# Norms of the delta rule as per-token scalars, its gate columns beside the rotary key, and two PSUM banks held in the RWKV scan

## What is computed

```python
q = l2_normalize(q) * 64 ** -0.5         # x * rsqrt(sum(x*x) + 1e-6), per token and head
k = l2_normalize(k)                      # 8 heads of 64
beta = sigmoid(gb); g = -exp(a_log) * softplus(ga + dt_bias)
gc = cumsum(g)                           # inside a chunk of 64 tokens
lhs = strict(einsum(k * beta, k) * exp(gc_i - gc_j)) + I
u, w = solve(lhs, v * beta), solve(lhs, k * beta * exp(gc))
o = einsum(q * exp(gc), S) + einsum(incl(q k^T * decay), v_new)
o = rms_norm(o, norm_w) * silu(gz)       # eps 1e-6, over 64
```

## Time and profile before

| | us |
|---|---|
| median of 3 runs (4081.65 to 4089.67) | 4083.42 |
| the profiled execution | 4090.37 |
| its span, first to last instruction | 4088.6 |

### The profile page before, as it was taken

How to read it: one execution, slowest core, us unless ns; L and a number is a source line. 1 busy time by engine, 2 the same in 40 slices (tenths; PEclk the granted TensorE clock), 3 DMA queues, 4 the chain that set the end, 5 groups by cost and what they waited for, 6 DMA issues and landing times.

```text
span 4088.6 us, 71017 instructions
## 1 busy us (share of the span) xinstructions
PE 3896.2 (95%) x30810; PEld 3170.3 (78%) x30810; DVE 2103.5 (51%) x2922; ACT 1309.5 (32%) x1891; POOL 144.6 (4%) x193
## 2 busy tenths in 40 slices
PE   8998978999999999999989999999999998999998
PEld 5766768887778888888768688887888767688887
DVE  4977466755444445334755453345333746553335
ACT  4253333213323323222422532223222332532222
POOL 0000012220000000000000000000000000000000
PEclk8999878999999999999999999999999989999999
DMA  6213000023342223333102032322323201123331
GB/s 253 71 63 99 7 2 3 3 72 140 124 134 99 93 97 99 103 93 103 53 3 82 11 109 93 103 98 88 103 93 104 63 12 57 37 88 103 93 103 52
DMA packets 319751, 327.81 MB, mean 80 GB/s; under 512 B 10064, under 2 KB 243552, under 8 KB 318032
## 3 DMA queue, kind: packets, MB, share of 16 engines
q1 hardware_dynamic: 312144, 287.01, 21.9%
q0 software_dynamic: 7296, 36.27, 2.4%
HBM read 314.86 MB, written 8.39 MB: 79 GB/s over the span
## 4 chain that ended last, share of the span: by engine, by line
PE 74%; issue 12%; DVE 9%; ACT 3%; DMA 1%; POOL 0%; DVEq 0%; ACTq 0%; SPq 0%; POOLq 0%
PE psum L247 72%; DVE arena L301 2%; PE psum L254 2%; ACT arena L351 1%; DVE arena L312 1%; DVE ring L301 1%; DVE r L301 1%; DVE ring L332 1%; ACT r L351 1%; ACT ring L351 1%; DVE arena L332 1%; DMA ring<-in_w_ada 0%; DVE ring L308 0%; DVE arena L316 0%; DVE arena L306 0%
## 5 line engine op out<-in xcount | busy, mean ns | idle before, releaser
L247 PE MATMUL psum<-r 128*128 128x512 f32 (+2 forms) x12960 | 2847.6, 381 | 30.6 <-DVE r L301 28.4
L247 PEld LDWEIGHTS psum<-r 128*128 128x128 f32 x12960 | 2343.7, 188 | 521.2 <-DVE r L301 28.5
L301 DVE TENSOR_TENSOR r<-ring,r 128x2048 fp32r<-128x2048 f32 (+2 forms) x261 | 573.7, 2198 | 322.3 <-ACT r L351 318.7
L351 ACT ACTIVATE r<-ring 128x2048 fp32r<-128x2048 f32 (+2 forms) x261 | 478.6, 1834 | 362.9 <-PE psum L247 310.4
L351 ACT ACTIVATE arena<-psum 128x512 f32<-128x512 f32 (+7 forms) x509 | 268.1, 527 | 999.5 <-PE psum L247 923.5
L247 PE MATMUL psum<-arena 64*64 64x64 f32 (+11 forms) x5854 | 486.6, 271 | 35.0 <-DVE arena L301 9.7
L247 PEld LDWEIGHTS psum<-arena 64*64 64x64 f32 (+5 forms) x5854 | 313.9, 155 | 175.9 <-issue 100.4
L301 DVE TENSOR_TENSOR arena<-arena,psum 128x512 f32<-128x512 f32 (+4 forms) x217 | 136.3, 628 | 582.5 <-PE psum L247 563.5
L247 PE MATMUL psum<-ring 64*64 64x64 f32 (+3 forms) x7792 | 302.5, 232 | 44.7 <-DVE ring L332 12.8
L247 PEld LDWEIGHTS psum<-ring 64*64 64x64 f32 (+2 forms) x7792 | 262.0, 142 | 68.8 <-issue 30.8
L351 ACT ACTIVATE r<-arena 128x512 fp32r<-128x512 f32 (+1 forms) x176 | 109.4, 622 | 503.0 <-DVE arena L301 500.8
(11 more groups left out here) (113 smaller groups left out, 1532.3 us busy)
## 6 DMA issues: line engine op xcount, KB each, us to landing
ring<-in_ffa_w_in SPq DMA_DIRECT2D x88, 512.0 KB, 4.7
ring<-in_ffb_w_in SPq DMA_DIRECT2D x88, 512.0 KB, 4.7
ring<-in_w_mlp SPq DMA_DIRECT2D x32, 1024.0 KB, 5.2
ring<-in_w_in SPq DMA_DIRECT2D x31, 1024.0 KB, 5.2
ring<-in_w_ada SPq DMA_DIRECT2D x24, 1024.0 KB, 5.2
ring<-in_mix_w_in SPq DMA_DIRECT2D x24, 1024.0 KB, 5.1
ring<-in_ffa_w_out SPq DMA_DIRECT2D x20, 1024.0 KB, 4.9
ring<-in_ffb_w_out SPq DMA_DIRECT2D x20, 1024.0 KB, 5.0
```

What stands on the lines that cost most here:

```text
L247: ins = self.raw.matmul(o, l, r, start=start, stop=stop, skip_group_check=True)
L301: self.done(self.raw and self.raw.tensor_tensor(o, a, b, f), keys)
L351: self.done(self.raw and self.raw.activation(o, i, f, scale=scale, bias=bias), keys)
```

## The change

1. **RWKV scan.** `K.held` is a set of banks that `take` passes over. From A's take until the tile's inverse begins, A's two banks are in it.
2. **Norms as scalars.** q and k stay unnormed. The squares are summed with the squares as the stationary side and a 128x2 table as the moving one, so the sums come per token (`m.sums`). ScalarE takes `lk` = ln(sum of k) and `rk` = exp(-lk/2). `rk` goes into beta's factor, `-lk/2` into the decay's exponents on the key's side (by a product with the new constant `steps` and two small operations), and q's norm into the epsilon of the output's norm (`m.eq`). The head table's transposes, the root, the reciprocal, `to_all` and `dve_mx_scale` go.
3. **Gate columns beside the rotary key.** One chunk `abkr` of 128 columns holds the 16 gate columns and the 64 of the rotary key; its 24 products stand where the gates' were. VectorE does the rotary there. The product `kr2` and its chunk go, and one `E.ahead()` on ScalarE and on VectorE with it.

```diff
     def take(self, *key, among=BANKS):
-        b = next(b for b in K.order if b in among)
+        b = next(b for b in K.order if b in among and b not in K.held)
...
+def rw_held(K, d, pos):
+
+    return {K.bank_of[f"rw{d}", "A", pos, g][0] for g in range(2)}
...
         o = [t.take(st, "A", pos, g) for g in range(2)]
+        K.held |= rw_held(K, d, pos)
...
     for pos in range(6):
+        K.held -= rw_held(K, d, pos)
         yield from pe_invert(t, K, f"rw{d}", K.m.rw[d].sets[pos % 2], pos, (f"rw{d}", "AT sb", pos))
...
 def pe_mx_in(E, K, l):
-    for q in (0, 1):
-        o = t.take("mx hb", l, q)
-        for i in range(4):
-            f = 4 * q + i
-            t.tr(o[0:16, 128 * i:128 * i + 128], C["hs"][:, 16 * f:16 * f + 16], *([("mx hb", l, q)] if i == 3 else []))
...
-            t.mm(sums[0:16, :], C["hs"][:, 16 * f:16 * f + 16], m.tmp2[f % 2], f == 0, f == 7, ("mx sums", l, f))
+            for i in range(4):
+                t.mm(sums[:, 16 * i + 2 * f:16 * i + 2 * f + 2], m.tmp2[f % 2][:, 128 * i:128 * i + 128], C["b2"][:, 0:2],
+                     True, True, *([("mx sums", l, f)] if i == 3 else []))
...
-    i, wh, wl = t.chunk(W, 0, 8, 2048, 16)
+    i, wh, wl = t.chunk(K.I["abkr"][l], 0, 8, 0, 128)
...
-    def to_all():
-        z = [K.bank_of[("mx z", l), 0, i][0] for i in range(4)]
-        for f in range(8):
-            o = t.take("mx rn", l, f, among=tuple(b for b in BANKS if b not in z))
-            t.wait_ge(*K.at("mx rn", l))
-            t.mm(o, m.hb[0:16, 128 * f:128 * f + 128], m.rn[0:16], True, True, ("mx rn b", l, f))
...
-    pe_tm(t, K, ("mx z", l), W, 1536, 512, 8, m.hL, W512, within=to_all, late=lambda: pe_gates(E, K, l))
+    pe_tm(t, K, ("mx z", l), W, 1536, 512, 8, m.hL, W512, late=lambda: pe_gates(E, K, l))
...
 def act_mx_in(E, K, l):
-    a.wait_ge(*K.at("mx sums sb", l))
-    a.act(m.rn[0:16], m.rn[0:16], ACT.Sqrt, ("mx sd", l))
...
 def dve_mx_in(E, K, l):
     v.wait_ge(*K.at("mx sums", l, 7))
-    v.ts(m.rn[0:16], K.bank("mx sums", l)[0:16, :], 1e-6, None, ADD, None, ("mx sums sb", l))
+    v.ts(view(m.sums, [1, 64]), K.bank("mx sums", l)[:, 0:64], 1e-6, None, ADD, None, ("mx sums sb", l))
...
-    v.recip(m.rn[0:16], m.rn[0:16], ("mx rn", l))
+    v.ts(m.eq, m.sums[:, :, 0:8], 64e-6, None, MUL, None)
+    v.wait_ge(*K.at("mx ab", l))
+    dve_rotary(v, m.tmp, m, m.krT[RP, :], K.bank("mx ab", l))
...
 def pool_gates(E, K, l):
+    g.load(m.steps, K.I["steps"], "steps", l)
...
 def dve_gates(E, K, l):
-    v.ts(m.ng, m.gg, -1.0, None, MUL, None)
+    v.wait_ge(*K.at("gd be", l))
+    v.tt(m.rk, m.rk, m.be, MUL)
...
 def dve_gates2(E, K, l):
-    v.tt(view(m.kde, [1, 32]), K.bank("gd gc", l)[:, 32:64], view(m.t8, [1, 32]), SUB, ("gd kde raw", l))
+    v.tt(view(m.kde, [1, 32]), K.bank("gd gc", l)[:, 32:64], view(m.t8, [1, 32]), SUB)
+    v.stt(m.kde, m.lk, -0.5, m.kde, MUL, ADD, ("gd kde raw", l))
+    v.stt(view(m.ng, [1, 32]), K.bank("gd gc", l)[:, 64:96], -0.5, view(m.gg, [1, 32]), MUL, SUB)
...
 def act_gates(E, K, l):
+    a.wait_ge(*K.at("mx sums sb", l))
+    a.act(m.lk, m.sums[:, :, 8:16], ACT.Ln, ("gd lk", l))
+    a.act(m.rk, m.lk, ACT.Exp, scale=-0.5)
...
 def pe_gates(E, K, l):
+    t.wait_ge(*K.at("gd lk", l))
+    t.wait_ge(*K.at("in", "steps", l))
+    t.mm(o[:, 64:96], m.steps, view(m.lk, [1, 32]), True, True, ("gd gc mm", l))
...
-    t.wait_ge(*K.at("mx qk", l, 7))
...
 def pe_sb_in(E, K, l):
-    i, wh, wl = t.chunk(K.I["kr2"][l], 0, 8, 0, 128)
-    o = t.take("sb kr", l)
-    for k in range(8):
-        t.mm3(o, wh[:, k, :], wl[:, k, :], m.hL[:, 0, k, :], m.hL[:, 1, k, :], k == 0, k == 7,
-              *([("sb kr", l), ("w used", i)] if k == 7 else []))
...
 def dve_sb_in(E, K, l):
-    E.ahead()
     dve_mla_squares(E, K, l, "c", m.ckv, m.small[:, 4:8], ("mla n", l, "var"))
     dve_mla_norm(E, K, l)
     E.ahead()
-    v.wait_ge(*K.at("sb kr", l))
-    dve_rotary(v, m, m.krT[RP, :], K.bank("sb kr", l))
```

More of the change, by code:

```diff
@@ L118, in __init__ @@
         self.psum = ctx.enter_context(nc.psum_tensor("psum", [128, 8, 512], F32))
-        self.operands, self.r = set(), {}
+        self.operands, self.r, self.held = set(), {}, set()
         self.restart()
@@ L922, in memory @@
     m.cv = view(al(1024), [512, 2], [1, 512])
-    m.rn, m.abT = al(512), al(512)
-    m.hb = view(m.ktok, [1, 1024])
+    m.steps = al(128)
+    al(384)
+    m.abT = al(512)
     A.top = mk6 + 336
     m.Og = view(al(2048), [512, 4], [1, 512])
-    A.top += 1024
+    m.sums = view(al(64), [16, 4], [1, 16])
+    m.lk, m.rk, m.eq = (view(al(32), [8, 4], [1, 8]) for _ in range(3))
+    A.top += 1024 - 160
     m.al_, m.dtb = al(8), al(8)
@@ L3079, in act_mx_in @@
     a.copy(m.abT[0:16], K.bank("mx ab", l)[0:16, :], ("mx ab sb", l))
-    K.free(a, "mx ab", l)
+    K.free(a, "mx ab", l, part="act")
     to_tokens(11)
-    a.wait_ge(*K.at("mx sums sb", l))
-    a.act(m.rn[0:16], m.rn[0:16], ACT.Sqrt, ("mx sd", l))
     for _ in tm_walk(E, 512, 8, 4):
@@ L3128, in dve_mx_in @@
         pass
-def dve_mx_scale(E, K, l):
-    v, m = VectorLine(E, "mx"), K.m
-    for f in range(8):
-        v.wait_ge(*K.at("mx rn b", l, f))
-        x, pv = m.qk[:, f, :], K.bank("mx rn", l, f)
-        if f < 4:
-            v.stt(x, x, 0.125, pv, MUL, MUL)
-        else:
-            v.tt(x, x, pv, MUL, ("mx qk", l, f))
-        K.free(v, "mx rn", l, f)
 def pool_gates(E, K, l):
@@ L3219, in pe_gates @@
     t.mm(o[:, 0:32], C["UI"], view(m.gg, [1, 32]), True, True)
[L3220 removed]
+    t.mm(o[:, 32:64], C["blk"], view(m.gg, [1, 32]), True, True)
+    t.wait_ge(*K.at("gd lk", l))
+    t.wait_ge(*K.at("in", "steps", l))
+    t.mm(o[:, 64:96], m.steps, view(m.lk, [1, 32]), True, True, ("gd gc mm", l))
     o = t.take("gd egl", l, among=others)
@@ L3525, in dve_gd_squares @@
         v.red(m.small[:, 8 * i:8 * i + 8], h8(m.tmp2[i % 2]), ADD)
-    v.ts(m.small[:, 0:32], m.small[:, 0:32], 1.0 / 64, 1e-6, MUL, ADD, ("gd n", l, "var"))
+    v.stt(m.small[:, 0:32], m.small[:, 0:32], 1.0 / 64, view(m.eq, [1, 32]), MUL, ADD, ("gd n", l, "var"))
 def dve_gd_out(E, K, l, i):
@@ L3547, in pe_gd_out, with dve_rotary @@
     pe_to_fm(TensorLine(E, "gd"), K, ("gd yT", l), [K.m.Og[:, i, :] for i in range(4)], 4, ("gd out", l, 3))
-def dve_rotary(v, m, o, x, *keys):
-    v.tt(m.tmpr[RP, :], x[RP, :], m.cosT[RP, :], MUL)
+def dve_rotary(v, tmp, m, o, x, *keys):
+    v.tt(tmp[RP, 0:512], x[RP, :], m.cosT[RP, :], MUL)
     v.tt(o, x[RS, :], m.sinT[RS, :], MUL)
-    v.tt(o, o, m.tmpr[RP, :], ADD, *keys)
+    v.tt(o, o, tmp[RP, 0:512], ADD, *keys)
 def pe_sb_in(E, K, l):
@@ L3855, in dve_mla @@
         v.wait_ge(*K.at("mla heads", l, n))
-        dve_rotary(v, m, m.qh[RP, n, :], K.bank("mla h", l, n, 0))
+        dve_rotary(v, m.tmpr, m, m.qh[RP, n, :], K.bank("mla h", l, n, 0))
         K.free(v, "mla h", l, n, 0, part="dve")
@@ L4221, in arrays_of @@
     a["uqs"] = np.ascontiguousarray(np.concatenate([u, u[..., 80:96], u[..., 64:80]], axis=-1).reshape(2, 256, 512))
-    r = g["mix_w_in_2"][:, :, 3216:3248]
-    z64 = np.zeros(r.shape[:2] + (64,), r.dtype)
-    a["kr2"] = np.ascontiguousarray(np.concatenate([z64, r, r[..., 16:32], r[..., 0:16]], axis=-1))
+    r, ab = g["mix_w_in_2"][:, :, 3216:3248], g["mix_w_in_2"][:, :, 2048:2064]
+    z48 = np.zeros(r.shape[:2] + (48,), r.dtype)
+    a["abkr"] = np.ascontiguousarray(np.concatenate([ab, z48, r, r[..., 16:32], r[..., 0:16]], axis=-1))
+    i, j = np.arange(128)[:, None], np.arange(128)[None, :]
+    a["steps"] = np.ascontiguousarray(1.0 * (i == j) - 1.0 * ((i + 1 == j) & (j % 64 != 0)), np.float32)
     a["consts"] = const_tables()[1]
```

12 lines of the change are left out of this document (4 added, 8 removed).

## The result

The changed kernel takes 4019.4 us (median of 4 runs, 4009.9 to 4027.1) where the kernel before takes 4082.5 (4 runs, 4079.3 to 4089.7): a ratio of 0.9842, 95% interval 0.9817 to 0.9867, so 63 us less. The forecast was 4028 us with a range of 4011 to 4047; the time lies in it, 9 us under the forecast. The profiled execution took 4017.63 us, 72.7 less than the profiled one of before.

What follows compares the result with a forecast made beforehand. TensorE, busy 95% of the span, was taken as the bound, with bank waits in the scan. 11.5 + 14.9 + 11.2 + 9.9 + 9 = 56.5 us, less 1.5 for the median, took 4083.4 to 4028 us; range 4011 to 4047.

Steps and rivals of the forecast that it cites:

- The eight waits: RWKV scan: TensorE waits for bank A of direction 0 or 1 in turn, 13.4 us in sum.
- Input stage: Delta rule's input stage: head, sums, norm spreading and small things give 11.5 us in layer 0, 14.9 in layer 1.
- sums of squares: Input stage: four products replace one fp32 product per job, saving 0.06 us a job, 0.5 a layer.
- head transposes: Head of the input stage: eight transposes of the head table go, saving 0.8 us a layer.
- Costed at nothing: Input stage: added VectorE and ScalarE work costs nothing; gates have over 5 us of cover before TensorE asks.
- Stage after the delta rule: Rotary key's 24 products go: 5.6 us a layer, 11.2 in all; 0.4 us slack ahead of the transposes.
- The scan's banks: Scan: holding A's banks wins 9.9 us of bank waits, bounds 0 and 13.4.
- The clock behind those waits: Scan: 27.5 us at half speed beside four waits lose 13.7 us; 9 come back, bounds 0 and 13.7.
- rival 2: Scan: waits and clock return whole, 65 us gained, time 4019 us; chance 0.18.
- Rival 1: Scan gives nothing back because VectorE or the turned copies end last, time 4046 us; chance 0.20.
- rival 3: Layers: cover fails at gates or squares' chain, or lower clock stays in projection; 4040 us at 6 a layer; chance 0.09.
- rival 4: Scan: slower, as the hold leaves six banks and products meet ones VectorE still reads; chance 0.03.

Runs made afterwards that it cites:

- `full_rows`: The kernel before, with the eight norm-spreading products per layer reading 128 rows (112 zeros) instead of 16: 4076.0 us, ratio 0.9982.
- `hold_only`: The kernel before with only the hold of A's two banks in the scan, layers unchanged: 4065.3 us, ratio 0.9948.
- `hold_mb`: The changed kernel with the masked products' two banks held as well until the same inverse: 4023.5 us, ratio 0.9856 to the kernel before.

## Why the prediction was right, and which terms were off

**What bounds the kernel.** Right: TensorE's list in the layers, and its waits for a bank in the scan. The eight waits ended with A's copies, as read: each direction's hold takes away its own.

**Input stage.** Forecast 11.5 and 14.9 us; the trace gives 13.3 and 16.7. The turning of the gate columns to the first decay product took 37.4 us (2032.99 to 2070.41) and 40.8 (3284.53 to 3325.30), and takes 27.1 in both layers: 10.3 and 13.7, where 10.1 less 0.2 and 13.5 less 0.2 stood. Counting the lower level of the projection with the thin products was right, and `full_rows` and the six projections that have them show it. The wait for the bank of the sums went from 0.55 to 0.33, 0.2 us for the 0.3 forecast. The mis-sized term is the sums of squares: 0.06 us a job, with 1.3 us a layer as the upper bound; it is 0.24 (6.63 to 6.39), 1.9 us a layer. I priced four products with two moving columns from a group that stands behind other products, and they are cheaper still (0.81 us, where I had 0.90); and I left out that the wide products behind a job follow closer. The head transposes gave 0.9 us for the 0.8 forecast: the way from the transposes among which they stood to the wait ahead of the first block took 9.51 us (1945.17 to 1954.68) and takes 8.64 (1911.64 to 1920.28).

**Costed at nothing.** The gates had 8.6 us of cover (forecast over 5) and the squares' chain 0.9 (0.4). The wait ahead of the first decay differences is 2.35 us as before, so the three small operations of VectorE cost nothing there.

**Stage after the delta rule.** From the stage's first product to the transposes it is 39.83 us (2150.47 to 2190.30), it was 45.31 (2200.84 to 2246.15): 5.5 us a layer, 11.0 in all, forecast 11.2.

**The scan's banks.** Forecast 9.9 us, measured 8.0 over all profiles, 7.9 in the pair and 8.7 in the part where the waits stand. Direction 0's waits keep 1.01 us (forecast 0.9). Of direction 1's, one keeps 0.80 us where I had said nothing is late next: the same wait for the turned copy.

**The clock behind those waits.** This term was the most off: forecast 9 us with 13.7 as the upper bound, measured 16.3 over all profiles and 21.1 in the pair. The step that failed is the partial return. I took two thirds, since a quarter of the waiting stays; but in the part of the scan where the waits stand nearly all of the lower level went (29.4 us at 0.50 on average with the banks in rotation, 0.5 with both held), though waits of 1.0 us stay there, and TensorE's busy time fell by 12.0 us. That the 27.5 us read from one profile lie near the mean of five is luck: the five have 23.9 to 44.4. What the pair has beyond that stands elsewhere, and I counted none of it: pieces at 631 us and between 914 and 935 us, with no wait of A's right ahead, went, and the one at 576.5 us shrank from 10.2 to 3.4. These also come and go without the hold.

By the rule of the Trainium skill ("TensorE: Matmul & The Clock Gate", "A second HAM failure mode: psum-queue depth-cycling"), short idles from cycling through banks are enough to swing the clock; on record with the forecast, all 13.7 us would then come back. The runs agree with it in the part where the waits stand. They also show it for idles that have nothing to do with banks (2.2 us for data).

**Sum.** By the trace 13.3 + 16.7 + 11.0 + 24.2 = 65 us, against 63 between the medians and 55 forecast. The banks gave 1.9 us less than forecast, the input stages 3.6 more and the clock 7.3 more, and 1.5 us had been taken off for the median. That the range held owes something to its width: it went past rival 2, and the sums of squares and, over the whole scan, the clock lay above their upper bounds. The outcome is rival 2, waits and clock whole (4019, chance 0.18), in its time; in its parts it is not quite: 8.0 of 13.4 us of waits, more clock, and 41.0 us in the layers where it had 37.6. Rival 1 falls with `hold_only`, rival 3 with the cover measured, rival 4 with `hold_mb`.

**Left open.** What the lower level at 914 to 935 us comes from isn't shown. Nor is why a wait of one length is followed by a stretch at 0.50 in one place and not in another: the wait of 2.35 us ahead of the first decay differences was followed by one in layer 1 of the changed kernel (at 3256.5 us), and not in layer 0.

## What to carry to other kernels

When a round-robin of banks hands out the one that its readers give back last, keep it out of the rotation until its own consumer has been built: the wait is then one for the data alone, and here more than half of the gain (12.0 of 20.7 us where the waits stand) came from the clock, which a sum over the wait view doesn't show. An fp32 product that uses few of TensorE's rows is not only unproductive; back to back, eight of them cost up to 1.4 us apiece, where 0.8 was enough with 128 rows, and the wide products behind them ran in part at half speed. Size a clock term over several profiled executions: one execution of the same scan differs from another by up to 8 us.

## What the hardware showed that was not expected

- Behind products of 16 rows, back to back, the granted clock went from 1.00 to 0.50 with TensorE busy throughout (kernel before); with 128 rows, 112 of them zeros, it stayed at 1.00 and the eight took 6.46 us instead of 8.79 and 11.00. With products of 8 rows ahead of the scan it is the same (the clock from 491.7 us on is 0.50 with 8 rows and 1.00 with 128).
- The clock's share follows each direction's waits by itself: where the eight waits stand, the lower level was granted for 29.4 us on average with both in rotation, 10.2 with one held and 0.5 with both.
- A wait of 2.20 us for data, with no bank in it, was followed by the lower level 28 times out of 28; of the 32 waits of 1.0 us in the scans with direction 0's banks held, none was.
